# Turning the forgetting heads' normalized results by 32x32 blocks and scratch memory in place of TensorE, in one core's encoder layer

## What is computed

```python
s = jnp.einsum('bqhd,bkhd->bhqk', q, k).astype(jnp.float32) * (HEAD_DIM ** -0.5)
s = s + jnp.transpose(c_q, (0, 2, 1))[..., :, None] - jnp.transpose(c_k, (0, 2, 1))[..., None, :]
p = jax.nn.softmax(jnp.where(mask, s, -jnp.inf), axis=-1)
fo = jnp.einsum('bhqk,bkhd->bqhd', p, v)
fo = rms_norm(fo, fox_norm_w_l).reshape(bsz, t_, FOX_WIDTH)
out = jnp.concatenate([fo, go.astype(fo.dtype)], axis=-1) @ w_out_l
```

## Time and profile before

| what | value |
|---|---|
| median of three runs | 1889.69 us (1888.07 to 1890.96) |
| the profiled execution | 1889.48 us, of it span 1887.9 us |
| TensorE busy | 1861.8 us, 99% |
| VectorE busy | 1076.7 us, 57% |
| ScalarE busy | 729.3 us, 39% |
| forgetting heads 0 to 7 beside their blocks | about 73 to 308 us of the span |

### The profile page before, as it was taken

One profiled execution on the slowest core, in us unless ns is written; L12 is line 12 of the kernel. 1 busy time (PEld: TensorE's weight loads), 2 busy tenths in 40 slices (PEclk: granted clock), 3 DMA queues, 4 the chain that ended last, 5 costly groups with the idle time before them and its releaser, 6 DMA issues.

```text
span 1887.9 us, 31205 instructions
## 1 busy us (share of the span) xinstructions
PE 1861.8 (99%) x9409; PEld 1577.3 (84%) x9409; DVE 1076.7 (57%) x2353; ACT 729.3 (39%) x1467; POOL 268.5 (14%) x491
## 2 busy tenths in 40 slices
PE   7999999999999999999999999999999999999997
PEld 6999998888888888888888888888888888888886
DVE  6666666888888874664545454433334444444455
ACT  4444344554555433343333333333333333333330
POOL 2343433333333310001111110000000000000000
PEclk9999999999999999999999999999999999999999
DMA  7666674444444335245556645544445555467441
GB/s 209 184 162 160 164 172 124 117 112 112 116 112 117 117 114 164 91 129 165 156 152 165 173 128 164 162 130 129 129 129 146 145 164 162 122 167 212 162 134 67
DMA packets 317413, 270.77 MB, mean 143 GB/s; under 512 B 96600, under 2 KB 230624, under 8 KB 316704
## 3 DMA queue, kind: packets, MB, share of 16 engines
q1 hardware_dynamic: 306880, 250.90, 47.4%
q0 software_dynamic: 10464, 18.99, 4.0%
HBM read 249.73 MB, written 20.06 MB: 143 GB/s over the span
## 4 chain that ended last, share of the span: by engine, by line
PE 97%; DVE 1%; DMA 1%; SPq 1%; issue 0%; ACT 0%; DVEq 0%; POOL 0%; ACTq 0%; POOLq 0%
PE bank L298 70%; PE bank L2033 9%; PE bank L1769 7%; PE bank L1885 2%; PE bank L1245 1%; PE bank L1227 1%; PE bank L1239 1%; PE bank L1221 1%; SPq L230 1%; DMA x_res<-in_x_sample 0%; PE bank L1195 0%; DMA raw<-in_w_in 0%; PE bank L640 0%; PE bank L1288 0%; PE bank L417 0%
## 5 line engine op out<-in xcount | busy, mean ns | idle before, releaser
L274 DVE TENSOR_TENSOR w_lo<-raw,w_hi 128x512 fp32r<-128x512 f32 (+2 forms) x828 | 565.3, 691 | 620.4 <-ACT w_hi L269 617.2
L269 ACT ACTIVATE w_hi<-raw 128x512 fp32r<-128x512 f32 (+2 forms) x828 | 502.6, 616 | 838.2 <-PE bank L298 700.8
L298 PE MATMUL bank<-w_hi,aT_hi 128*128 128x512 f32 (+2 forms) x1776 | 695.7, 392 | 2.0 <-DVE aT_lo L432 1.6
L298 PE MATMUL bank<-w_hi,aT_lo 128*128 128x512 f32 (+2 forms) x1776 | 673.2, 379 | 0.0
L298 PE MATMUL bank<-w_lo,aT_hi 128*128 128x512 f32 (+2 forms) x1776 | 672.1, 378 | 0.0
L298 PEld LDWEIGHTS bank<-w_hi,aT_hi 128*128 128x128 f32 x1776 | 334.4, 188 | 60.3 <-issue 9.4
L298 PEld LDWEIGHTS bank<-w_hi,aT_lo 128*128 128x128 f32 x1776 | 333.7, 188 | 55.4
L298 PEld LDWEIGHTS bank<-w_lo,aT_hi 128*128 128x128 f32 x1776 | 334.7, 188 | 47.4
L298 PE MATMUL bank<-w_hi,hT_hi 128*128 128x512 f32 x288 | 112.0, 389 | 0.0
L298 PE MATMUL bank<-w_lo,hT_hi 128*128 128x512 f32 x288 | 112.0, 389 | 0.0
L298 PE MATMUL bank<-w_hi,hT_lo 128*128 128x512 f32 x288 | 112.0, 389 | 0.0
(11 more groups left out here) (366 smaller groups left out, 1986.8 us busy)
## 6 DMA issues: line engine op xcount, KB each, us to landing
raw<-in_ffn_w_gate SPq DMA_DIRECT2D x176, 256.0 KB, 2.7
raw<-in_ffn_w_up SPq DMA_DIRECT2D x176, 256.0 KB, 2.7
raw<-in_ffn_w_down SPq DMA_DIRECT2D x176, 256.0 KB, 3.3
raw<-in_w_in SPq DMA_DIRECT2D x128, 192.0 KB, 2.4
raw<-in_w_in SPq DMA_DIRECT2D x128, 128.0 KB, 2.3
raw<-in_w_in SPq DMA_DIRECT2D x256, 64.0 KB, 2.3
raw<-in_w_out SPq DMA_DIRECT2D x61, 256.0 KB, 3.2
h_blocks<-sg SPq DMA_DIRECT2D x11, 768.0 KB, 4.5
```

Of the source, the lines that this page charges most:

```text
L269: nc.scalar.activation(w_hi[:, g % RING, 0:width], raw[:, g % RAW, 0:width], ACT.Copy).then_inc(sem("w_high"), 1)
L274: nc.vector.tensor_tensor(w_lo[:, g % RING, 0:width], raw[:, g % RAW, 0:width], w_hi[:, g % RING, 0:width], ALU.subtract).then_inc(sem("w_ ...
L298: last = nc.tensor.matmul(acc[t][:, 0:width], l[:, k0 + n, t * P:(t + 1) * P], r[:, g % RING, 0:width], start=(n == 0 and j == 0), stop=(n ...
```

## The change

For heads 0 to 6 TensorE no longer turns `fo`. VectorE, behind its scaling and a wait on its own result (`after`), turns the 384 columns of `fo` by blocks of 32x32 into `fturn`, which is the first part of the tile `sc`, and signals `f_o`. SyncE stores `fturn` to the memory `turns` ahead of its ninth load of the body, and loads it back with the blocks moved into `fmoved`, the first part of the tile `pT`, ahead of its eleventh, in four transfers, when the store has landed. In the next head ScalarE writes `mixF_hi` of the head before at slot 8, when the four have landed, and VectorE `mixF_lo`, ahead of adding the key rows. Head 7 stays with TensorE. `F_OWN` counts the waits of `after` in a head.

```diff
-F_OWN = 14
+F_OWN = 15
+TURN_STORE_AT, TURN_LOAD_AT, TURN_MIX_AT = 9, 11, 8
@@
+            turns = nc.dram_tensor("turns", (TOK, HD), F32, kind="Internal").ap()
+            def turned_by_pe(h):
+                return isinstance(h, int) and h == HEADS - 1
+            def store_turned(sp, tile, ready, count):
+                sp.wait_ge(sem(ready), count)
+                sp.dma_start(turns.rearrange("(t p) f -> p t f", p=P), tile).then_inc(sem("o_stored"), 16)
+            def load_moved(sp, tile, h):
+                sp.wait_ge(sem("o_stored"), 16 * (h + 1))
+                for r in range(4):
+                    sp.dma_start(
+                        tile[SQUARE * r:SQUARE * (r + 1), :].rearrange("b (a c) -> b a c", c=SQUARE),
+                        turns.rearrange("(a b) (r c) -> b r a c", b=SQUARE, r=4)[:, r]).then_inc(sem("o_moved"), 16)
@@
+                fturn = sc[:].rearrange("p t c -> p (t c)")[:, 0:TOK]
+                fmoved = pT[:].rearrange("p t c -> p (t c)")[:, 0:TOK]
@@ fox_pe
-                    yield 41 + min(later, FIRST_TURN_LATER)
-                    W("f_o")
-                    for t in range(TT):
-                        last = nc.tensor.transpose(b3[:, t * P:(t + 1) * P], fo[:, t, :], ident)
-                    last.then_inc(sem("f_oT_ps"), 1)
-                    yield 45 + later
-                    W("f_mix")
+                    if turned_by_pe(h):
+                        yield 41
+                        W("f_o")
+                        for t in range(TT):
+                            last = nc.tensor.transpose(b3[:, t * P:(t + 1) * P], fo[:, t, :], ident)
+                        last.then_inc(sem("f_oT_ps"), 1)
+                        yield 45
+                        W("f_mix")
@@ fox_act
+                    else:
+                        yield TURN_MIX_AT
+                        act.wait_ge(sem("o_moved"), 64 * h)
+                        nc.scalar.activation(mixF_hi[:, bass.ds(h - 1, 1), :], fmoved.unsqueeze(1), ACT.Copy,
+                                             scale=nwf[:]).then_inc(sem("f_mix_hi"), 1)
@@
-                    yield 41 + min(later, FIRST_TURN_LATER)
-                    W("f_oT_ps")
+                    if not turned_by_pe(h):
+                        return
+                    yield 41
+                    act.wait_ge(sem("f_oT_ps"), 1)
@@ fox_dve
+                        dve.wait_ge(sem("f_mix_hi"), h)
+                        nc.vector.scalar_tensor_tensor(
+                            out=mixF_lo[:, bass.ds(h - 1, 1), :], in0=fmoved.unsqueeze(1), scalar=nwf[:],
+                            in1=mixF_hi[:, bass.ds(h - 1, 1), :], op0=ALU.mult, op1=ALU.subtract)\
+                            .then_inc(sem("f_mix"), 1)
@@
+                    if not turned_by_pe(h):
+                        after(last)
+                        nc.vector.transpose(fturn, fo[:].rearrange("p t c -> p (t c)"))\
+                            .then_inc(sem("f_o"), 1)
+                        assert own[0] == F_OWN
+                        return
+                    own[0] += 1
@@ fox_sp
+                    def next_turn(n, h):
+                        if n == TURN_STORE_AT:
+                            store_turned(sp, fturn.rearrange("p (t c) -> p t c", t=TT), "f_o", h + 1)
+                        if n == TURN_LOAD_AT:
+                            load_moved(sp, fmoved, h)
                     with sp.Fori(0, HEADS - 2) as i:
                         for n in range(NP_IN):
+                            next_turn(n, i)
                             loads(sp, 2 * NP_IN + n + NP_IN * i, n % RAW, fox_parts(i + 2, n, n % RAW))
                     for n in range(NP_IN):
+                        next_turn(n, HEADS - 2)
                         loads(sp, G_GDN + n, n % RAW, gdn_parts(0, n, n % RAW))
```

## The result

| | before | changed |
|---|---|---|
| median of the timed runs | 1889.69 us | 1894.68 us |
| the profiled execution's span | 1887.9 us | 1894.3 us |
| ratio, with its 95% interval | | 1.0028 (1.0018 to 1.0037) |

The change makes the kernel slower: the medians differ by 5.0 us, and the ratio says 0.28%. One of the eleven executions of the changed kernel took 3139.12 us at a granted clock of 0.557, where the other ten have 0.996 to 0.998; the ratio is taken without it, and without it the median is 1894.44 us, 4.7 above before's. The forecast was 1892.2, the range 1887.0 to 1899.5: sign and range held, the size was 2.7 us where 5.0 came. By the prediction's own line (above 1893.5) the kernel is slower, to which it had given a chance of 0.36.

A forecast was written before the change was run, and what follows sets the result against it. TensorE, busy 99% of the span, was taken as the bound, with VectorE's chain level with it once a head. Head 0 -0.5, VectorE's turn +1.7, late landing +0.5 and head 1 +1.0 gave +2.7: 1892.2 us, range 1887.0 to 1899.5.

The forecast's parts named there:

- The bound: Forgetting stage: TensorE is full, and VectorE's chain is level with it at weight piece 13, held 0.11 us each head.
- The turn removed: TensorE's three turns of fo go in seven heads: 0.33 us a head, 2.3 us in all.
- VectorE's turn: Added ahead of piece 13's low split: 0.61 us a head, net +0.28 in heads 1 to 6, +1.7 us.
- Head 0 and head 1: Head 0: -0.5 us in sum. Head 1: +0.28 from VectorE's turn, and +1.0 from blocks landing late.
- The steady late landing: Moved blocks reach VectorE 1.58 us late in the next head: 0.1 us for each of heads 2 to 6, +0.5.
- the free time: Room before VectorE's lateness from the moved blocks reaches TensorE: 1.30 us, or up to 1.45 as instructions overlap.
- rival (a): Moved blocks land late by much, TensorE waiting at piece 9: +7 us, 1899, or +20 us, 1912; chance 0.32.
- (b): VectorE's turn is covered, piece 13 waits 0.11 us as before, landing in time: -2.5 us, 1887.0; chance 0.12.
- (c): Each TensorE turn costs its whole duration, 272 ns: 21 give 5.7 us, 1883.8 with VectorE covered; chance 0.04.

The follow-up runs named there:

- e8: The kernel before, with VectorE's three scalings by the inverse root moved behind the low split of piece 13: 1888.46 us, ratio 0.9995.
- e2: The kernel before, with VectorE's wait and 32x32 turn added in heads 0 to 6, result unused, TensorE still turning: 1893.21 us, ratio 1.0019.
- e1: The kernel before, with TensorE's turns left out in heads 0 to 6, a price only since the layer's result is not right: 1886.46 us, ratio 0.9984.
- e9: e5 with VectorE's wait on its own scaling also moved behind the low split of piece 13: 1886.49 us, ratio 0.9985.
- e10: The changed kernel, with GpSimd's four stores of k and v held back until VectorE has added the key rows: 1891.83 us, ratio 1.0011.
- e3: The changed kernel, with the store ahead of SyncE's load 6 and the four loads ahead of load 8, not 9 and 11: 1890.18 us, ratio 1.0003.
- e7: The changed kernel, with the four loads ahead of SyncE's load 12 in place of 11: 1903.95 us, ratio 1.0074.
- e5: The changed kernel with e3's earlier store and loads, and VectorE's turn behind the low split of piece 13: 1887.91 us, ratio 0.9991.

## Why the prediction came out as it did

**The bound, right.** The place where VectorE's chain stood level with TensorE was read from one step of 0.28 us that the list of waits leaves out; e8 and e2 show it from both sides.

**The turn removed, right.** 0.33 us a head; e1 gives 0.31 to 0.37 in heads 2 to 6, 0.34 in the mean.

**VectorE's turn, right.** Forecast 0.61 in the chain; the trace has 0.62, its instruction 0.58 long, and e2 alone gives +3.84 for the stage where +3.7 was expected.

**Head 0 and head 1, right.** Forecast -0.5 and +1.3 (0.28 + 1.0). Measured, by the starts of the first products: head 0 took 21.29 us in place of 21.60, and head 1 31.25 in place of 30.17. As before's block behind head 0 began with a late first product (0.10, now gone), that is -0.4 and +1.2: each is 0.1 off, and the two cancel.

**The steady late landing, mis-sized.** The term "0.1 us for each of heads 2 to 6, +0.5" measured 0.31 us in head 2 and 0.53 or 0.54 in heads 3 to 6, 2.5 in all. It had been set under the 0.13 to 0.28 of its own working, in the hope for issues closer than 0.57 us. These five heads took 30.60, 30.95, 30.84, 30.83 and 30.81 us in place of 30.04 to 30.06, together +3.8 us where +1.9 was forecast (5 x 0.38). This is the error of the sum. The mechanism, the free time and the place (piece 9) were as forecast.

The landing was not: 2.1 us was taken from raw loads late in a block, when these loads run beside GpSimd's stores, where the last of each four took 2.75 to 2.90. The issues did come closer, 0.50 to 0.52 us apart, and SyncE began them sooner, so that the last was issued 4.0 to 4.1 us behind the block's first product in place of 4.45; this hid a part of the longer landing, and the earlier start was luck. In heads 3 to 6 the last load landed at 6.82 to 6.96, where 217.4 less 210.85, 6.55, was forecast, and in head 2 at 6.60. From there to VectorE's start it took 0.94 us, where 0.86 was counted. So VectorE stood 1.93 to 2.07 us late, not 1.58. Of this 1.4 to 1.5 was free, the upper end of the forecast's 1.30 to 1.45. The page's rows for out<-fbuf had been read for their price, but not for their time: they start as the blocks' loads do. The period of 30.84 lies between the 30.3 to 30.5 of the forecast and the 31 from which rival (a) was to hold, nearer to the rival: part of (a) came, for a reason that it did not name, and what spoke for it, the small runs, had no part.

**The rivals (b) and (c)** fell with e2 and e1. The warning of the Trainium skill ("VectorE: DVE Perf Modes", the three transpose paths) of strided copies was rightly left aside for runs of 128 B: away from GpSimd's stores they land in 2.2 us, as the raw loads do (2.1 us in the earlier trace rows). And the rule of the Trainium skill ("VectorE: DVE Perf Modes", the rules for kernel authors) to turn 128x128 on TensorE doesn't hold in this stage, where TensorE is full and VectorE isn't: in e9 the way round TensorE is worth the whole price of the turns (237.16 us, against 237.15 with no turn at all).

**What stays open.** The medians differ by 5.0 us and the stages by 4.5; whether 0.5 belongs to the change was not separated from the scatter ahead of the stage. Why head 2 of e10 issued its loads later (its store took 2.67 us to land, where the other steady heads' took 2.16 to 2.27) and was held longer at piece 13 was not tried.

## What to carry to other kernels

Where one engine is busy all the time, count what is ahead of each hand-over to it, and look at single steps of 0.1 us. In this kernel, work moved onto a half idle engine cost its full length where it stood ahead of a hand-over that was level, and nothing one instruction later. Place a trip through memory by when its last transfer lands, with the landing taken from transfers that run beside the same neighbours, other queues' included.

## What the runs showed of the hardware

A load of 48 KB in runs of 128 B landed 2.1 to 2.2 us (medians) from its issue away from another queue's stores (e3, e7, e10), as the raw loads of 64 KB in runs of 512 B do (2.1 us), and 2.7 us beside four stores of GpSimd's queue (changed kernel). VectorE's wait for its own preceding result took 0.2 us more than going on with independent work (0.80 in e5 against 0.60 in e9, behind the same three scalings). Three 128x128 turns of fp32 cost a TensorE that is never idle 0.33 us together (e1), though each is 0.27 long. VectorE's turn of 128x384 in 32x32 blocks is 0.58 us long, and the next instruction starts 0.50 behind it (209.53 to 210.03).
